# One bias product instead of sixteen, window attention scored one unit ahead, and a second early weight tile lowered after the norm

## The chip, the cores and the metric

The kernel is written in Bass for one core of a Trainium2 chip. It is one launch, and the metric is its device time in microseconds (us). The kernel before takes 3031.45 us, the median of three runs from 3026.38 to 3034.74. Five engines work beside one another and meet at semaphores: PE multiplies matrices, DVE and ACT do elementwise work, reductions and functions, POOL and SP here mostly issue DMAs.

## The reference, cut to what matters

The program computes two transformer blocks one after the other on 256 tokens of 1024 features. The first (`first_block`) has two layers, each a token mixer of three attention branches and a gated feed-forward with a convolution. The second has a gated delta-rule mixer, a SwiGLU feed-forward, a sliding-window attention with sinks and a bias by relative distance, and a mixture of eight experts with two chosen per token. The change touches the window attention and the two places where one stage hands over to the next.

```python
def swa_sink_attention(x, w_in, b_in, sinks, rel_bias, w_out):   # 16 query heads of 64, 2 key heads
    proj = x @ w_in + b_in
    ...
    s = jnp.einsum('bnqkgd,bnskd->bnkgqs', q, kb).astype(jnp.float32) * (SWA_HEAD_DIM ** -0.5)
    dist = qi + SWA_BLOCK - kj
    bias = rel_bias[t5_bucket(jnp.maximum(dist, 0))]             # rel_bias: 32 buckets x 16 heads
    band_ok = (dist >= 0) & (dist < SWA_WINDOW)                  # window of 128
    s = jnp.where(mask, s + bias, -jnp.inf)
    p = jax.nn.softmax(jnp.concatenate([s, sink], axis=-1), axis=-1)[..., :-1]
    o = jnp.einsum('bnkgqs,bnskd->bnqkgd', p, vb).reshape(bsz, t, SWA_QDIM)
    return o @ w_out
# between stages: x = layernorm(ALPHA * x + y); h = x * (1 + sc) + sh; next product h @ w
```

## The kernel before, in words

**Weights.** Every large product is made in three passes, so that it keeps fp32 accuracy on a faster format. A weight tile of 128x2048 comes from memory into one of four slots of `W` (SP issues the load), ACT copies it to a rounded "high" part (`raise_weight`, L1535), DVE subtracts to get the "low" part (`lower_weight`, L1953, two halves of 128x1024 per tile), and PE runs high x high, high x low, low x high (`product`, L805 to L807). PE hands the slot back when the tile is used. All engines run through the list of tiles in one order written by hand: `high(n)` and `low(n)` say where in ACT's and DVE's program the next n tiles are taken. At the end of a layer the first two tiles of the next stage are raised and lowered ahead of time, into free places of `arena` (`high_next`, `low_next(part, 2)`); the next stage's own list on DVE then starts behind these two.

**Handing over.** After the last product of a feed-forward (`down`, four results of 128x512), DVE adds each to x (`residual`), takes statistics, normalises (`norm`), PE transposes x in sixteen 128x128 pieces, and DVE and ACT scale and split the transposed x (`shifted` and `high_shifted`, two groups of four pieces, q = 0 and 1). Behind that DVE scales x itself (`scale_x`, four operations), and goes on to the next weight tiles. `shifted` takes a function that it calls after each group.

**The bias rows.** The bias of a head depends on the distance alone, so one row of 384 numbers per head describes it. In the middle stage, between the `up` and `down` products of the SwiGLU, PE multiplies for each of the 16 heads a 32x128 matrix, in which the head's 32 bucket values are repeated over 128 columns (`relspread`, made by DVE), with a 32x384 one-hot table. This gives the row 128 times. DVE adds the mask row to each (`add_row`, sixteen times, into `relw`). POOL writes the result, 16 heads x 128 partitions x 384 numbers, to `spread` in memory (L779), waits, and reads it back with a pitch of 383 per partition (L782), so that partition p gets the row shifted by p. The result is `wbias`; DVE waits for it (`bias_in`) before the window attention.

**The window attention.** There are 16 units: eight pairs of heads x two token blocks. The block t = 0 has 128 keys, the block t = 1 has 256. PE's program is, per unit u, the two score products of unit u (L980), the transposes of the probabilities of unit u-1 (L999), and the products with the values of unit u-2 (L1012). DVE's is: scale and bias the two score matrices of u (L2235), take the row maxima (L2241), take the maximum with the sinks, negate, subtract from the sinks (L2244, L2246, L2248), wait for ACT's exponentials of the same unit (L1596), add the sink's term and invert (L2997, L2999), and scale the result of unit u-2 (`w_out`, L2987). ACT's is: the exponential of the sinks (L1593), the two exponentials of unit u with their row sums, and the copy of the transposed probabilities of u-1 (L1520). `scores` and the small per-unit tiles have two buffers.

Banks of PSUM are given out in the order in which PE's program asks for them, eight in rotation; `JOBS` holds how many each stage uses.

## Time and profile before

| | |
|---|---|
| Time, median of three runs | 3031.45 us |
| The profiled execution | 3030.37 us, its span 3028.6 us |
| PE busy | 2732.2 us (90%) |
| DVE busy | 2177.5 us (72%) |
| ACT busy | 1508.3 us (50%) |
| Chain that ended last | PE 43%, DVE 21%, weight loads of PE 17%, issue 8%, ACT 7%, DMA 3% |
| Sixteen bias products | from 1729.14, 18.12 us |
| Window attention | from 1858.92 to 1929.49, 70.57 us |
| Residual after `down`, stage before layer 1 | starts at 691.37 |
| The same before the middle stage | starts at 1316.06 |

Times are counted from the start of the span. A matmul of PE is recorded with the weights and data that it reads; in full fp32 one product is recorded as two matmuls, so the sixteen bias products are 32. A busy PE is not a PE at its peak; the column PEclk gives the clock that the chip granted it, 1.00 for 2.4 GHz and 0.50 for 1.2 GHz. "[1.50 <-DVE small L2999]" behind a row means that the engine had been idle for 1.50 us until the DVE instruction of that line was done.

### The profile page before, as it was taken

To read this page: it belongs to the slowest core of one execution; us is meant where nothing else is said; L and a number is where in the kernel's file an instruction comes from. 1 tells how busy PE (TensorE), PEld (TensorE's weight loads), DVE (VectorE), ACT (ScalarE), POOL (GpSimd) and SP (SyncE) were. 2 spreads that over 40 slices of the span, in tenths; PEclk is the share of its full clock that TensorE was granted. 3 is DMA by queue.
4 is the path that set the end of the run, shared out by engine and by line. 5 is a ranking of instruction groups with operands and counts; after the bars stand their busy time and mean duration, and the time that the engine had idled before them with its cause. 6 is when DMAs were issued, how large, how long until landed. Compare 5 with 4: busy or idle time off the path is not lost.

```text
span 3028.6 us, 38615 instructions
## 1 busy us (share of the span) xinstructions
PE 2732.2 (90%) x14170; PEld 2319.9 (77%) x14170; DVE 2177.5 (72%) x2757; ACT 1508.3 (50%) x1773; POOL 24.4 (1%) x46
## 2 busy tenths in 40 slices
PE   8988798898887889987989997779999999999997
PEld 8777678886766679877889975668888888888886
DVE  1766577778756677665676646578889898898987
ACT  1333434533334345435333334447777777777774
POOL 0000000000000000000000000000000000000000
PEclk7989899999989999987999997679999999999999
DMA  6743345576633355442114462249889998898985
GB/s 248 271 165 135 119 156 205 205 262 244 228 129 125 114 192 204 166 148 85 56 56 164 167 234 86 98 180 367 338 339 362 343 368 337 336 363 342 370 336 222
DMA packets 104714, 671.13 MB, mean 222 GB/s; under 512 B 11984, under 2 KB 12240, under 8 KB 27136
## 3 DMA queue, kind: packets, MB, share of 16 engines
q1 hardware_dynamic: 97584, 622.08, 55.5%
q0 software_dynamic: 6992, 47.19, 4.2%
q8 instruction: 89, 1.46, 0.2%
q14 instruction: 49, 0.40, 0.0%
HBM read 665.03 MB, written 4.19 MB: 221 GB/s over the span
## 4 chain that ended last, share of the span: by engine, by line
PE 43%; DVE 21%; PEld 17%; issue 8%; ACT 7%; DMA 3%; PEldq 0%; DVEq 0%; ACTq 0%; SPq 0%
PE bank L805 12%; PE bank L806 11%; PE bank L807 11%; DVE W_low L1953 7%; PEld bank L807 5%; PEld bank L805 5%; PEld bank L806 5%; ACT W_high L1535 3%; PE bank L1189 3%; PE bank L939 2%; DMA W<-in_w_expert 2%; PE bank L862 1%; DVE work L2020 1%; PEld bank L1419 1%; DVE scores L2235 1%
## 5 line engine op out<-in xcount | busy, mean ns | idle before, releaser
L1953 DVE TENSOR_TENSOR W_low<-W,W_high 128x1024 fp32r<-128x1024 f32 x426 | 496.7, 1207 | 350.7 <-ACT W_high L1535 347.4
L1535 ACT ACTIVATE W_high<-W 128x1024 fp32r<-128x1024 f32 x426 | 421.8, 1039 | 479.4 <-PE bank L807 240.7
L806 PE MATMUL bank<-W_low,arena_parts 128*128 128x512 f32 x1288 | 506.5, 393 | 0.0
L805 PE MATMUL bank<-W_high,arena_parts 128*128 128x512 f32 x968 | 388.3, 401 | 10.1 <-DVE W_low L1953 5.8
L807 PE MATMUL bank<-W_high,arena_parts 128*128 128x512 f32 x968 | 381.9, 395 | 0.0
L807 PE MATMUL bank<-hT_high,W_low 128*128 128x256 f32 x1184 | 340.6, 288 | 0.0
L805 PE MATMUL bank<-hT_high,W_high 128*128 128x256 f32 x1072 | 312.4, 291 | 16.7 <-DVE W_low L1953 8.6
L805 PE MATMUL bank<-W_high,hT_high 128*128 128x512 f32 (+3 forms) x680 | 280.6, 413 | 35.6 <-DVE W_low L1953 12.1
L806 PE MATMUL bank<-hT_low,W_high 128*128 128x256 f32 x1072 | 307.5, 287 | 0.0
L806 PE MATMUL bank<-W_low,hT_high 128*128 128x512 f32 (+4 forms) x720 | 286.1, 397 | 0.0
L806 PEld LDWEIGHTS bank<-W_low,arena_parts 128*128 128x128 f32 x1288 | 244.4, 190 | 49.2
L805 PE MATMUL bank<-arena_parts 128*128 128x512 f32 x672 | 272.6, 406 | 1.9 <-DVE arena_parts L3110 1.9
L807 PE MATMUL bank<-W_high,hT_low 128*128 128x512 f32 (+3 forms) x680 | 270.1, 397 | 0.0
L807 PE MATMUL bank<-arena_parts 128*128 128x512 f32 x672 | 263.7, 392 | 0.0
L807 PEld LDWEIGHTS bank<-hT_high,W_low 128*128 128x128 f32 x1184 | 232.9, 197 | 0.0
L805 PEld LDWEIGHTS bank<-hT_high,W_high 128*128 128x128 f32 x1072 | 209.5, 195 | 23.5 <-DVE W_low L1953 13.5
L806 PE MATMUL bank<-arena_parts 128*128 128x512 f32 x576 | 225.5, 391 | 0.0
L805 PEld LDWEIGHTS bank<-W_high,arena_parts 128*128 128x128 f32 x968 | 184.4, 191 | 53.0 <-DVE W_low L1953 8.8
L1582 ACT ACTIVATE arena_parts<-W 128x2048 fp32r<-128x2048 f32 x96 | 184.3, 1920 | 76.5 <-DMA W<-in_w_expert 59.7
L1987 DVE TENSOR_TENSOR W_low<-W,arena_parts 128x2048 fp32r<-128x2048 f32 x96 | 218.0, 2285 | 2.8 <-ACT arena_parts L1582 2.8
L807 PEld LDWEIGHTS bank<-W_high,arena_parts 128*128 128x128 f32 x968 | 183.8, 190 | 40.1
L806 PEld LDWEIGHTS bank<-hT_low,W_high 128*128 128x128 f32 x1072 | 209.9, 196 | 0.1
(375 smaller groups left out, 4724.7 us busy)
## 6 DMA issues: line engine op xcount, KB each, us to landing
W<-in_w_expert SPq DMA_DIRECT2D x192, 1024.0 KB, 4.8
W<-in_w_layer SPq DMA_DIRECT2D x170, 1024.0 KB, 4.9
arena<-in_w_expert SPq DMA_DIRECT2D x144, 1024.0 KB, 4.8
W<-in_w_middle SPq DMA_DIRECT2D x58, 1024.0 KB, 4.8
arena<-in_w_layer POOLq DMA_DIRECT2D x40, 1024.0 KB, 6.1
R<-in_rows_layer SPq DMA_DIRECT2D x70, 256.0 KB, 5.8
R<-in_rows_middle SPq DMA_DIRECT2D x18, 256.0 KB, 5.5
spread<-arena POOLq DMA_DIRECT2D x1, 3072.0 KB, 13.7
```

Source lines behind the costliest of these rows:

```text
L805: mm(bank, lhs[0], rhs[0], start=start, stop=False)
L806: mm(bank, lhs[0], rhs[1], start=False, stop=False)
L807: return mm(bank, lhs[1], rhs[0], start=False, stop=stop)
L862: last = turn_over(bank[:, i * P:(i + 1) * P], src[:, t, f:f + P], ident)
L939: last = mm(bank[:, n:n + 1], part[:, a_:a_ + P], csil[:, f:f + 1], start=k == 0, stop=k == 3)
L1189: last = mm(bank[:, i * P:(i + 1) * P], lhs(i), rhs(i), start=True, stop=True)
L1419: last = turn_over(bank[:, i * P:(i + 1) * P], hid_tok[:, c % 2, i * P:(i + 1) * P], ident)
L1535: do(high_slot(at, w)[:, cols], raw(at, w)[:, cols], ACT.Copy).then_inc(main_highs.filled[main_highs.slot(at, w)], 1)
L1582: do(expert_high(j), expert_raw(j), ACT.Copy).then_inc(stream.raised, 1)
L1953: tt(lows(at, w)[:, cols], raw(at, w)[:, cols], high_slot(at, w)[:, cols].bitcast(F32), ALU.subtract).then_inc(*low_ready.event(at))
L1987: tt(expert_low(j), expert_raw(j), expert_high(j).bitcast(F32), ALU.subtract).then_inc(stream.lowered, 1)
L2020: i = stt(acc, part, csil[:, f:f + 1], acc, ALU.mult, ALU.add)
```

## The change

**Bias rows.** PE makes one product for all heads: the 32x16 table of bucket values as it came from memory against the one-hot table, 16x384. DVE adds the mask row once, on 16 partitions. The repetition over 128 partitions moves into the DMA that writes `spread`, whose source is now a broadcast of 16 partitions. `relspread` and its copy are gone.

**Window attention.** PE makes the scores of unit u+1 before it transposes the probabilities of u-1, DVE masks unit u+1 before it waits for the exponentials of unit u. Scores and the small tiles get three buffers of their own (`wscores`, `wmax`, `wsum`, `wsink`). DVE takes the maxima negated and takes the minimum with negated sinks, which were made once, so one of the three small operations is gone; ACT no longer waits between its three exponentials.

**Second early tile.** `low_next` lowers one tile ahead of time and no longer two. The second is lowered by `shifted` behind its second group (`low(q)` with q = 1), for layer 1 and for the middle stage. ACT still raises both early.

```diff
@@ the bias rows: POOL, PE, DVE
-            pool.dma_start(spread.rearrange("h p m -> p h m"), relw).then_inc(bias_out, 16)
+            pool.dma_start(spread, relrow[0:WQ_HEADS, :].unsqueeze(1).to_broadcast([WQ_HEADS, P, 384])
+                           ).then_inc(bias_out, 16)
...
-            for h_ in range(WQ_HEADS):
-                pe.wait_ge(*psum.vacant(at, ("rel", h_)))
-                bank = banks[psum.slot(at, ("rel", h_))]
-                mm(bank[:, 0:384], relspread[0:BUCKETS, h_, :], R[0:BUCKETS, hot, 0:384],
-                   start=True, stop=True).then_inc(*psum.fills(at, ("rel", h_)))
+            bank = banks[psum.slot(at, ("rel", 0))]
+            mm(bank[0:WQ_HEADS, 0:384], R[0:BUCKETS, relb, 0:WQ_HEADS], R[0:BUCKETS, hot, 0:384],
+               start=True, stop=True).then_inc(*psum.fills(at, ("rel", 0)))
...
-            for h_ in range(WQ_HEADS):
-                add_row(("rel", h_), r, relw[:, h_, :], width=384)
+            tt(relrow[0:WQ_HEADS, :], bank[0:WQ_HEADS, 0:384], r[0:WQ_HEADS, 0:384], ALU.add
+               ).then_inc(*psum.frees(v.at, ("rel", 0)))
@@ the window attention: PE
+            window_scores(0)
+            for u in range(16):
+                if u < 15:
+                    window_scores(u + 1)
+                if u:
+                    window_T(u - 1)
+                if u > 1:
+                    window_out(u - 2)
@@ ACT
+            def window_exps(u):
+                act.wait_ge(*masked.nth(a.at, u + 1))
+                K, b = (u % NT + 1) * P, u % 3
+                do(wsink[:, b, :], wsink[:, b, :], ACT.Exp)
+                for m in range(2):
+                    i = do(wscores[:, b, m, 0:K], wscores[:, b, m, 0:K], ACT.Exp,
+                           bias=wmax[:, b, m:m + 1], accum_out=wsum[:, b, m:m + 1])
+                i.then_inc(*exped.event(a.at))
@@ DVE
+            def window_mask(u):
+                hp, t = divmod(u, NT)
+                K, b = (t + 1) * P, u % 3
+                for m in range(2):
+                    job = ("Ws", hp, t, m)
+                    dve.wait_ge(*psum.full(v.at, job))
+                    bank = banks[psum.slot(v.at, job)]
+                    stt(wscores[:, b, m, 0:K], bank[:, 0:K], WD ** -0.5, wbias[:, 2 * hp + m, 2 * P - K:2 * P],
+                        ALU.mult, ALU.add).then_inc(*psum.frees(v.at, job))
...
+                V.reduce_max(wmax[:, b, :], wscores[:, b, :, 0:K], axis=AX, negate=True).then_inc(dve_done, 1)
+                tt(wmax[:, b, :], wmax[:, b, :], negative[:, 2 * hp:2 * hp + 2], ALU.min).then_inc(dve_done, 1)
+                tt(wsink[:, b, :], wmax[:, b, :], sinks[:, 2 * hp:2 * hp + 2], ALU.add).then_inc(*masked.event(v.at))
...
+            window_mask(0)
             for u in range(16):
-                mask("W", hp, t, u, 2, WD ** -0.5, lambda m, K: wbias[:, 2 * hp + m, 2 * P - K:2 * P])
+                if u < 15:
+                    window_mask(u + 1)
                 dve.wait_ge(*exped.nth(v.at, u + 1))
@@ the second early tile: DVE, end of layers 0 and 1, start of layer 1 and of the middle stage
-                low_next(LAYERS[l + 1] if l + 1 < DEPTH else "middle", 2)
+                low_next(LAYERS[l + 1] if l + 1 < DEPTH else "middle", 1)
...
-                    shifted("hT", modc[:, 80:88], modc[:, 88:96])
+                    shifted("hT", modc[:, 80:88], modc[:, 88:96], lambda q: low(q))
...
-            shifted("gxT", modc[:, 48:56], modc[:, 56:64])
+            shifted("gxT", modc[:, 48:56], modc[:, 56:64], lambda q: low(q))
```

DVE at the end of the middle stage's `up`, before; `arena<-bank,R` is the addition of the mask row, `W_low` a half of a weight tile lowered, `x<-x,bank` the residual after `down`:

```order
L2184 TENSOR_TENSOR acted<-acted,bank 128x256
L2186 CAST arena_parts<-acted 128x256
L2188 TENSOR_TENSOR arena_parts<-acted,arena_parts 128x256
L1943 TENSOR_TENSOR arena<-bank,R 128x384 x16
L1953 TENSOR_TENSOR W_low<-W,W_high 128x1024 x18
L1953 TENSOR_TENSOR W_low<-W,h_parts 128x1024 x2
```

The same of the changed kernel (its line numbers are its own):

```order
L2198 TENSOR_TENSOR acted<-acted,bank 128x256
L2200 CAST arena_parts<-acted 128x256
L2202 TENSOR_TENSOR arena_parts<-acted,arena_parts 128x256
L2947 TENSOR_TENSOR arena<-bank,R 16x384
L1967 TENSOR_TENSOR W_low<-W,W_high 128x1024 x18
L1967 TENSOR_TENSOR W_low<-W,h_parts 128x1024 x2
```

Sixteen additions on 128 partitions have become one on 16; the lowered tiles behind it stay.

PE in the window attention, before, two units from the third on; L980 are scores, L999 transposes, L1012 products with the values:

```order
L980 MATMUL bank<-arena 128x256 x2
L999 MATMUL bank<-consts,scores 128x128 x2
L1012 MATMUL bank<-arena,probsT 128x64 x4
L980 MATMUL bank<-arena 128x128 x2
L999 MATMUL bank<-consts,scores 128x128 x4
L1012 MATMUL bank<-arena,probsT 128x64 x2
```

The same of the changed kernel, with scores now at L981, transposes at L1000, products with the values at L1013:

```order
L981 MATMUL bank<-arena 128x128 x2
L1000 MATMUL bank<-consts,arena 128x128 x2
L1013 MATMUL bank<-arena,probsT 128x64 x4
L981 MATMUL bank<-arena 128x256 x2
L1000 MATMUL bank<-consts,arena 128x128 x4
L1013 MATMUL bank<-arena,probsT 128x64 x2
```

Before, the scores of a block with 256 keys stand ahead of the transposes of the unit just before it; now the scores of the block after that one (128 keys) stand there, one unit further ahead. The transposes read `wscores` in the arena.

DVE at the start of layer 1, before; `hT` and `hT_low` are the scaled and split transposes, `x<-x,R` is `scale_x`:

```order
L1973 TENSOR_SCALAR hT<-bank,modc 128x128 x4
L1980 TENSOR_TENSOR hT_low<-hT,hT_high 128x4x128 x2
L2146 TENSOR_TENSOR x<-x,R 128x2x512
L2148 TENSOR_TENSOR x<-x,R 128x2x512
L2146 TENSOR_TENSOR x<-x,R 128x2x512
L2148 TENSOR_TENSOR x<-x,R 128x2x512
L1953 TENSOR_TENSOR W_low<-W,W_high 128x1024 x2
```

The same of the changed kernel:

```order
L1987 TENSOR_SCALAR hT<-bank,modc 128x128 x4
L1994 TENSOR_TENSOR hT_low<-hT,hT_high 128x4x128 x2
L1967 TENSOR_TENSOR W_low<-W,arena_parts 128x1024 x2
L2160 TENSOR_TENSOR x<-x,R 128x2x512
L2162 TENSOR_TENSOR x<-x,R 128x2x512
L2160 TENSOR_TENSOR x<-x,R 128x2x512
L2162 TENSOR_TENSOR x<-x,R 128x2x512
L1967 TENSOR_TENSOR W_low<-W,W_high 128x1024 x2
```

The two halves of the second early tile (`W_low<-W,arena_parts`) now stand between the last split and `scale_x`; ahead of the residual they are gone. The middle stage has the same move.

## Rows read from the trace of the kernel before

**Rows 1.** The page, busy time of the engines.
```profile
PE 2732.2 (90%) x14170; PEld 2319.9 (77%) x14170; DVE 2177.5 (72%) x2757; ACT 1508.3 (50%) x1773; POOL 24.4 (1%) x46
```

**Rows 2.** Timeline of all engines around the bias products.
```profile
1729.14 18.12 PE L1338 MATMUL bank<-R,h 32*128 32x384 f32 x32 [0.30 <-PE bank L807]
1730.26 2.36 DVE L1953 TENSOR_TENSOR W_low<-W,W_high 128x1024 fp32r<-128x1024 f32 x2 [2.29 <-ACT W_high L1535]
...
1733.78 5.29 DVE L1943 TENSOR_TENSOR arena<-bank,R 128x384 f32<-128x384 f32 x9
...
1747.19 0.80 PE L805 MATMUL bank<-W_high,arena_parts 128*128 128x512 f32 x1
...
1752.43 0.39 PE L805 MATMUL bank<-W_high,arena_parts 128*128 128x512 f32 x1
1752.66 0.39 PE L806 MATMUL bank<-W_low,arena_parts 128*128 128x512 f32 x1
```

**Rows 3.** Busy time by stretch: stretch, length, busy PE, PEld, DVE, ACT, POOL, clock, DMA.
```profile
1733.00:1737.00 4.00, 4.00 (x8) 2.15 (x7) 3.76 (x8) 0.00 (x0) 0.00 (x0) 0.50 0.03 12
1747.00:1752.00 5.00, 5.00 (x12) 3.81 (x12) 0.56 (x1) 0.00 (x0) 1.18 (x1) 0.50 0.38 140
```

**Rows 4.** The tile `spread`: POOL's issue of the write, and both DMAs.
```profile
L779 POOL DMA_DIRECT2D spread<-arena x1: 1181/1181/1181, 1748.3 to 1748.3; - x1
...
DMA to landing us min/median/max: 12.2/13.0/13.7
```

**Rows 5.** Timeline of all engines, window attention: its start, two units, its end.
```profile
1858.92 0.93 PE L980 MATMUL bank<-arena 64*128 64x128 f32 x8 [0.88 <-ACTq L1523]
...
1870.73 0.69 PE L999 MATMUL bank<-consts,scores 128*128 128x128 f32 x2 [0.43 <-DVE small L2999]
...
1871.04 0.88 DVE L2235 SCALAR_TENSOR_TENSOR scores<-bank,arena 128x256 f32<-128x256 f32 x2
...
1874.84 0.16 DVE L2997 TENSOR_TENSOR small<-small 128x2 f32<-128x2 f32 x1 [1.61 <-ACT scores L1596]
...
1875.56 0.62 DVE L2235 SCALAR_TENSOR_TENSOR scores<-bank,arena 128x128 f32<-128x128 f32 x2
...
1877.06 0.16 DVE L2248 TENSOR_TENSOR small<-R,small 128x2 f32<-128x2 f32 x1
...
1929.49 3.68 PE L862 MATMUL bank<-consts,arena 128*128 128x128 f32 x16 [0.60 <-DVEq L3006]
```

**Rows 6.** Busy time by stretch, as rows 3: four units of the window attention.
```profile
1870.70:1887.30 16.60, 12.08 (x52) 9.58 (x52) 9.51 (x36) 7.14 (x25) 0.00 (x0) 0.50 0.00 0
```

**Rows 7.** Timeline of DVE, end of layer 0 and start of layer 1.
```profile
684.88 2.36 DVE L1953 TENSOR_TENSOR W_low<-W,arena_parts 128x1024 fp32r<-128x1024 f32 x2 [0.82 <-ACT arena_parts L1535]
689.09 2.36 DVE L1953 TENSOR_TENSOR W_low<-W,arena_parts 128x1024 fp32r<-128x1024 f32 x2 [1.85 <-ACT arena_parts L1535]
691.37 0.68 DVE L2164 TENSOR_TENSOR work<-bank,arena 128x512 f32<-128x512 f32 x1
...
710.04 1.22 DVE L2146 TENSOR_TENSOR x<-x,R 128x1024 f32<-128x1024 f32 x1
...
715.07 2.36 DVE L1953 TENSOR_TENSOR W_low<-W,W_high 128x1024 fp32r<-128x1024 f32 x2
```

**Rows 8.** Timeline of PE, the same place.
```profile
691.99 0.39 PE L807 MATMUL bank<-W_high,arena_parts 128*128 128x512 f32 x1
701.49 3.40 PE L862 MATMUL bank<-consts,x 128*128 128x128 f32 x16 [9.11 <-DVE x L2130]
706.39 0.47 PE L805 MATMUL bank<-arena_parts,hT_high 128*128 128x512 f32 x1 [1.50 <-DVE hT_low L1980]
...
717.54 0.40 PE L805 MATMUL bank<-W_high,hT_high 128*128 128x512 f32 x1
```

**Rows 9.** Timeline of DVE, end of layer 1 and start of the middle stage.
```profile
1313.78 2.36 DVE L1953 TENSOR_TENSOR W_low<-W,arena_parts 128x1024 fp32r<-128x1024 f32 x2 [2.17 <-ACT arena_parts L1535]
```

**Rows 10.** Timeline of PE, the same place.
```profile
1320.14 0.39 PE L807 MATMUL bank<-W_high,arena_parts 128*128 128x512 f32 x1
```

More of the change, by code:

```diff
@@ L129 @@
 ARENA = 22544
-JOBS = {'start': 0, 'layer0': 200, 'layer1': 192, 'middle': 281, 'expert': 37, 'last': 35, 'over': 37, 'end': 0}
+JOBS = {'start': 0, 'layer0': 200, 'layer1': 192, 'middle': 266, 'expert': 37, 'last': 35, 'over': 37, 'end': 0}
 GIVEN = {
@@ L2259, in _ @@
                 state["std"] = 0
-                state["group"], state["split"] = 0, iter(SPLIT[LAYERS[l]][2 if l else 0:])
+                state["group"], state["split"] = 0, iter(SPLIT[LAYERS[l]][1 if l else 0:])
                 if not l:
@@ L2655, in _ @@
             v.enter("middle")
-            state["std"], state["group"], state["split"] = 0, 0, iter(SPLIT["middle"][2:])
-            shifted("gxT", modc[:, 48:56], modc[:, 56:64])
+            state["std"], state["group"], state["split"] = 0, 0, iter(SPLIT["middle"][1:])
+            shifted("gxT", modc[:, 48:56], modc[:, 56:64], lambda q: low(q))
             for n in range(2):
```

81 lines of the change are left out of this document (34 added, 47 removed).

## Prediction, made before the changed kernel ran

> **What bounds the kernel now.** I read the page first, to see which engine is full. PE is busy for 90% of the span, DVE for 72%, ACT for 50% [rows 1]. This says that a saving counts where PE itself loses work, or where PE waits. It does not say which: the shares are means over many stages. So I went to the three places that the diff touches and read each from the timeline, asking what PE does there and what ends its waits.
>
> At the bias products PE doesn't wait, it works: 32 recorded matmuls take 18.12 us, from 1729.14, and the next product (`down`) starts at 1747.19 [rows 2]. During them the granted clock is 0.50, with PE busy for all of the stretch; it is still 0.50 while `down` begins [rows 3]. DVE's sixteen additions run beside them [rows 2]. So PE is the bound of this stretch and the products are a pure addition to the time.
>
> In the window attention PE is busy 12.08 us in 16.60 us for four units, DVE 9.51, ACT 7.14 [rows 6]. No engine is full: the unit goes round a ring. DVE masks unit u, waits 1.61 us for ACT's exponentials of that same unit, inverts, and only then does PE transpose [rows 5]. The period is 16.60 / 4 = 4.15 us per unit, and it is a latency. The clock is 0.50 here too.
>
> At the two handovers PE waits for DVE. Before layer 1 it is idle 9.11 us until the normalised x is there [rows 8]. DVE reaches the residual at 691.37 only after lowering two early tiles, and it had stood 1.85 us idle for ACT ahead of the second [rows 7]. Before the middle stage the second tile also has DVE idle first, for 2.17 us [rows 9].
>
> **The bias rows.** Removed on PE are 15 of 16 products, 30 of 32 recorded matmuls. The two that stay cost 2 x 18.12 / 32 = 1.1 us, so `down` can start at 1729.14 + 1.1 = 1730.3 instead of 1747.19: 16.9 us. It needs its first tile lowered, and DVE is then already at the next one, done at 1730.26 + 2.36 = 1732.6 [rows 2]; PE asks for that tile after 24 matmuls of 0.23 us (the distance of the last two rows of rows 2), at 1735.8. Further on the loads, ACT and DVE are paced by the slots that PE hands back, as before. Second, `down` began on the slow clock: its first 12 matmuls took 1752.43 - 1747.19 = 5.24 us, against 12 x 0.23 = 2.76 at the full clock, 2.5 us more. The product ahead, `up`, ran up to 1729, so with two sparse matmuls between I expect the clock to stay. Sum 16.9 + 2.5 = **19.4 us**; it is 16.9 if the clock falls all the same, and at most 20.6 if the two matmuls vanish.
>
> DVE loses fifteen additions, hidden behind PE today and worth nothing on their own; that the sixteenth works on 16 partitions is worth nothing either. The copy into `relspread` is hidden in the same way. The bucket row is released later than before, but its successor in that slot is a row for the norm after `down`.
>
> What the change adds is in the DMA. The write of `spread` now reads 16 partitions 128 times over; no row of the trace shows such a source. It can be issued at about 1733.78 + 0.6 = 1734.4 and its reader is DVE at the start of the window attention, at 1858.92 - 19.4 = 1839.5 in the new time [rows 2, 5]. So 105 us cover it and the reading back, which take 13.7 and at least 12.2 us now [rows 4]. POOL has nothing queued behind these two. Bounds: no quicker than nothing, which gives nothing since it is hidden, and free up to 105 - 13.7 = 91 us for the write, nearly seven times today's. I take zero. It shares the DMA engines with the weights of `down`, and did so before.
>
> The Trainium skill ("SBUF — State Buffer", section on the DMA port swizzle) speaks against this edit: partitions 0 to 15 reach only four of sixteen ports, measured there at 104 GB/s. The write moves 3.1 MB, so an estimate from that page is 30 us. With it the sum stays the same, since the cover is larger; no run here shows it yet.
>
> **The window attention.** Work per engine and unit in the new order, from the same rows. DVE's mask for 256 keys goes from 1871.04 to 1874.84 - 1.61 = 1873.23, 2.19 us; for 128 keys from 1875.56 to 1877.06 + 0.16 = 1877.22, 1.66 us [rows 5]. One of three small operations goes, at 0.2 us each, which leaves 1.99 and 1.46. Sum, reciprocal and `w_out` together take 1875.56 - 1874.84 = 0.72 us. The mean is (1.99 + 1.46) / 2 + 0.72 = 2.45 us a unit. ACT has 7.14 / 4 = 1.8, PE 12.08 / 4 = 3.02 [rows 6]. The ring is open: while ACT does unit u, DVE masks u+1, and PE has the scores of u+1 behind it. With a unit of distance more, the probabilities of u are ready some 3.5 to 4 us after its scores, and PE comes to transpose it two turns, 6 us, later. So the longest engine sets the pace: PE, 3.02 us.
>
> The start: the first mask can begin about 0.6 us after the start, masks 0 and 1 end at 4.1, unit 0 is inverted at 4.5, mask 2 ends at 6.0, unit 1 is ready for its transposes at 6.4. From there PE has work without a gap. Of its 16 x 3.02 = 48.3 us it has then done the scores of four units and one transpose, and the last product stands behind a wait; together about 6.5. That leaves 41.8, to 48.2. The last copy of probabilities, the last products, and `w_out` follow with about 3.3 us, as they do today. The total is 51.5 us instead of 1929.49 - 1858.92 = 70.57 [rows 5]: **19.1 us**. Bounds: zero, if every unit still closes its ring, and 24.5, if PE were not the longest: then DVE sets 2.45 us for 14 units, and 6.4 + 34.3 + 4.4 for the end gives about 45 to 46. I take 19.1 because the PE row is the one measured in this very loop, at the clock that it had there.
>
> About this clock the skill ("TensorE: Matmul & The Clock Gate", Part 1) says that throttling is the resting state and sustained activity of PE lifts it. That would give the attention the full clock once its gaps close, and the result of 24.5. The trace doesn't follow the plain form of it: in rows 3 PE is busy 4.00 of 4.00 us at 0.50. I keep it as a rival.
>
> **The second early tile.** Before layer 1, DVE is free at 684.88 + 2.36 = 687.2 and can start the residual 4.1 us earlier than 691.37. The four results of `down` are there when asked for: PE ends at 692.4 [rows 8] and finishes one every 12 x 0.23 = 2.76 us, so 684.1, 686.9, 689.6, 692.4; DVE takes about 2.2 us each and comes to the last at 694. The normalised x comes 4.1 us earlier, and the idle 1.85 us is gone. The 2.36 us of lowering now stand behind the last split, ahead of `scale_x` and whatever is queued there. PE needs the second tile's first half after 24 matmuls from 706.39 - 4.1, at 707.8; DVE has it at 710.04 - 4.1 + 1.2 = 707.1. That holds by 0.7 us. The next tile comes later relative to PE: it starts at 715.07 - 4.1 + 2.36 = 713.3, its first half is there at 714.5, and PE wants it at 717.54 - 4.1 = 713.4 [rows 7, 8]. PE waits 1.1 us. The gain is 4.1 - 1.1 = **3.0 us**. If DVE bounds what follows it is only the idle time, 1.85; if the wait is recovered, 4.1.
>
> Before the middle stage the first early tile is tiny, and DVE is free at 1313.78 - 2.17 = 1311.6. The last result of `down` comes at 1320.5 [rows 10], so there DVE starts the fourth residual instead of at 1316.06 + 3 x 2.2 + 0.3 = 1322.9. That is **2.4 us**. The lowering behind the split then eats what DVE has won, and `scale_x` ends when it does now; PE starts with a narrow product that uses the other tile. I take all of it, with zero as the lower end, if a step of DVE behind `scale_x` is what the stage waits for.
>
> **Sum.** 19.4 + 19.1 + 3.0 + 2.4 = 43.9 us. All of it lies ahead of the experts, whose loads SP issues only after the attention's result is split, so nothing behind can give it back or absorb it: the later part moves as a whole. 3030.37 - 43.9 = 2986.5 for the profiled execution, which lay 1.1 us under the median of the runs: 2987.5. I say **2987 us**.
>
> **The rivals.**
> 1. The clock rises in the attention (the rule above). For it: PE will have no gaps there, and its products use all 128 rows more often than the bias products did. Against: rows 3. It gives 24.5 instead of 19.1, so 2982.
> 2. The attention's period stays well above PE's work, say 3.6 us, since one of PE's in-order waits still falls on a late engine. For it: DVE's 2.45 leaves out most semaphore time. Against: 0.6 us of room per unit. 14 x 0.6 = 8 us less: 2995.
> 3. The handovers give nothing: DVE or row loads bound both starts. For it: layer 1 goes straight on at DVE at 715.07 without a pause [rows 7]. 5.4 us less: 2993.
> 4. Slower than before: the write from sixteen partitions chokes the DMA engines while `down` needs its weights. `down` uses a tile every 24 x 0.23 = 5.5 us over eleven tiles. If the write took eight times its 13.7 us, 110 us, and halved the rate of the weight loads throughout, each tile would come 5 us late, 55 us in all: 2987 + 55 = 3042. It turns the sign once the write costs `down` over 44 us. For it: the source has an eighth of the partitions. Against: the write before shared the engines with the same loads and PE ran on, and only a source slower than anything in the trace reaches this.
>
> **How the numbers follow.** Forecast 0.53, rival 1 0.2, rival 2 0.12, rival 3 0.1, rival 4 0.03, something else 0.02. The forecast and rivals 1 to 3 lie between 2982 and 2995; with the bounds of the terms (16.9 for the bias, 4.1 at layer 1) and the 4 us by which runs of this kernel differ from their median, the range is 2976 to 3001. A change within 0.3%, 9 us, is what I count as none; it takes the loss of four fifths of the sum, 0.02. Slower has rival 4 and a little for the unknown, 0.03. Faster 0.95.
>
> **What would show it.** One L1338 group of two matmuls, `down` starting within 2 us behind it at clock 1.00; PE's transposes in the attention with idle times near zero and a period near 3.0, or 2.5 with the clock at 1.00; the attention 51 to 52 us long; the residual before layer 1 starting 4 us earlier relative to the end of `down`, then about 1 us of PE waiting for `W_low` at the third tile; the write of `spread` landing long before DVE asks. The prediction is wrong if the attention keeps DVE idle for ACT, if `down` shows gaps on weight loads, or if a stretch behind the attention grows.

## The result, and the profile after

The changed kernel takes 2992.8 us (median of 4 runs, 2990.95 to 3003.66), the kernel before beside it 3029.4 us (median of 4, 3026.38 to 3034.74). The ratio is 0.988, its 95% interval 0.987 to 0.990: 1.2% faster. The forecast was 2987 us in a range of 2976 to 3001. The profiled execution took 2991.22 us (span 2989.4) against 3030.37 (span 3028.6): 39.2 us less, where the sum of the terms said 43.9.

Since both executions are timelines of the same work, the difference can be split at points that both have. Such a point is a product that starts a stage.

| stretch, and the points it runs between | before, us | after, us | difference | forecast |
|---|---|---|---|---|
| start to the first product of layer 1 | 706.39 | 701.22 | -5.2 | |
| layer 1, to the late wait inside its `down` | 603.86 | 605.07 | +1.2 | |
| (these two together) | | | -4.0 | -3.0 |
| handover to the middle, from there to its first product | 24.61 | 22.10 | -2.5 | -2.4 |
| middle, up to the bias products | 394.28 | 393.15 | -1.1 | 0 |
| bias products, `down`, projections, up to attention | 129.78 | 116.49 | **-13.3** | **-19.4** |
| window attention | 70.57 | 50.19 | -20.4 | -19.1 |
| attention's output to the first expert product | 74.20 | 74.11 | -0.1 | 0 |
| experts and end | 1024.9 | 1027.1 | +2.2 | 0 |

Of the first row 0.5 us was there before anything in the program differed. Three terms are as forecast within some 1.3 us. One is short by 6.1 us, and 2.2 us come back at the end. The 1.1 us of the middle stage were in no term.

The page, busy time of the engines, as [rows 1]:

```profile
PE 2714.3 (91%) x14140; PEld 2309.3 (77%) x14140; DVE 2162.2 (72%) x2726; ACT 1504.7 (50%) x1773; POOL 24.2 (1%) x46
```

PE has lost 30 matmuls and 18 us of work; the other 21 us are idle time. Now the bias rows, timeline of all engines, the place of [rows 2] (start, length, engine and line, then the operation; in brackets the idle time ahead and what ended it):

```profile
1721.54 0.80 PE L1338 MATMUL bank<-R 32*16 32x384 f32 x2 [0.30 <-PE bank L808]
1722.27 0.50 PE L806 MATMUL bank<-W_high,arena_parts 128*128 128x512 f32 x1
...
1726.17 0.55 DVE L2947 TENSOR_TENSOR arena<-bank,R 16x384 f32<-16x384 f32 x1
1727.07 1.05 POOL L779 DMA_DIRECT2D spread<-arena  x1 [542.60 <-DVEq L2950]
...
1744.85 0.50 PE L806 MATMUL bank<-W_high,arena_parts 128*128 128x512 f32 x1 [0.51 <-DVE W_low L1967]
...
1754.31 0.50 PE L806 MATMUL bank<-W_high,arena_parts 128*128 128x512 f32 x1 [3.71 <-DVE W_low L1967]
...
1755.40 0.63 PE L807 MATMUL bank<-W_low,arena_parts 128*128 128x512 f32 x1
1755.83 0.63 PE L808 MATMUL bank<-W_high,arena_parts 128*128 128x512 f32 x1
```

Two matmuls stand where 32 stood, and `down` starts 0.73 us behind the first of them, on the full clock. So far this is the forecast. But inside `down` PE now waits 0.51 and 3.71 us for a lowered weight tile; there was no such wait at these places before. Behind the second wait the products are 0.43 us apart instead of 0.23. Busy time by stretch (stretch, length, busy PE, PEld, DVE, ACT, POOL, then the granted clock, DMA busy share, GB/s), as [rows 3]:

```profile
1722.40:1732.00 9.60, 9.60 (x43) 7.91 (x44) 6.32 (x8) 3.39 (x5) 1.05 (x1) 1.00 0.60 143
1742.00:1752.00 10.00, 8.09 (x35) 6.04 (x33) 2.36 (x2) 2.07 (x3) 0.00 (x0) 1.00 1.01 245
1752.00:1762.00 10.00, 7.69 (x27) 6.08 (x28) 4.25 (x4) 3.95 (x4) 0.00 (x0) 0.83 0.99 256
```

What DVE waited for is ACT, and what ACT waited for stands in the waits of 1722 to 1792 (engine, tile and line, what it waited for, us in total, times, longest):

```profile
DVE W_low L1967 <- ACT W_high L1543: 35.8, 10, 7.1
POOL arena L783 <- DMA spread<-arena: 35.0, 1, 35.0
ACT W_high L1543 <- DMA W<-in_w_middle: 22.3, 4, 7.5
```

ACT waited 22.3 us for weight loads. In the view of before that starts with its `down` (1747 to 1812), ACT's waits were 27.4 us for PE and none for a load. The DMAs between 1727 and 1763 show the reason (packets of each queue, MB, share of the 16 DMA engines; issues with KB and median us to landing):

```profile
q0 software_dynamic: 704, 3.15, 63.4%
q1 hardware_dynamic: 642, 4.74, 31.2%
...
W<-in_w_middle SPq DMA_DIRECT2D x6, 1024.0 KB, 17.0
spread<-arena POOLq DMA_DIRECT2D x1, 3072.0 KB, 35.8
```

and of before, 1748.3 to 1762, the write of the same 3 MB:

```profile
q0 software_dynamic: 704, 3.15, 67.7%
q1 hardware_dynamic: 133, 1.02, 19.9%
...
spread<-arena POOLq DMA_DIRECT2D x1, 3072.0 KB, 13.7
```

The write takes 35.8 us instead of 13.7 [rows 4]. Its packets held the engines for 0.634 x 36 x 16 = 365 engine-microseconds, against 0.677 x 13.7 x 16 = 148 before, for the same bytes. The loads' own packets did not get dearer: 0.312 x 36 x 16 / 4.74 = 38 engine-microseconds per MB, against 0.199 x 13.7 x 16 / 1.02 = 43 before. So the write is not only late itself: while it runs, a weight load lands in 17.0 us, and the loads get 4.74 MB / 36 us = 132 GB/s where `down` uses one tile of 1.05 MB in some 5.44 us, 193 GB/s.

Window attention, timeline of PE, one pair of units:

```profile
1852.40 0.69 PE L1000 MATMUL bank<-consts,arena 128*128 128x128 f32 x2
1852.88 1.80 PE L1013 MATMUL bank<-arena,probsT 128*128 128x64 f32 x8
1854.61 1.23 PE L981 MATMUL bank<-arena 64*128 64x256 f32 x4
1855.77 1.11 PE L1000 MATMUL bank<-consts,arena 128*128 128x128 f32 x4
1856.67 0.95 PE L1013 MATMUL bank<-arena,probsT 128*128 128x64 f32 x4
1857.56 0.80 PE L981 MATMUL bank<-arena 64*128 64x128 f32 x4
1858.29 0.69 PE L1000 MATMUL bank<-consts,arena 128*128 128x128 f32 x2
```

and busy time by stretch, 16.6 us of it, as [rows 6]:

```profile
1852.40:1869.00 16.60, 16.60 (x76) 13.61 (x74) 11.20 (x44) 8.49 (x35) 0.00 (x0) 0.50 0.00 1
```

No transpose here carries a wait, where the one of [rows 5] waited 0.43 us for DVE; in the whole stage those of two units wait, of sixteen before. A pair takes 1858.29 - 1852.40 = 5.89 us instead of 8.30; PE is busy all of it, at clock 0.50. At the two handovers PE's rows, as [rows 8, 10], are:

```profile
696.52 3.48 PE L863 MATMUL bank<-consts,x 128*128 128x128 f32 x16 [4.65 <-DVE x L2144]
701.22 0.47 PE L806 MATMUL bank<-arena_parts,hT_high 128*128 128x512 f32 x1 [1.23 <-DVE hT_low L1994]
...
713.45 0.50 PE L806 MATMUL bank<-W_high,hT_high 128*128 128x512 f32 x1 [0.94 <-DVE W_low L1967]
...
728.30 0.79 PE L806 MATMUL bank<-W_high,hT_high 128*128 128x512 f32 x1 [2.28 <-DVE W_low L1967]
...
1319.96 2.22 PE L863 MATMUL bank<-consts,x 128*128 128x128 f32 x16 [3.39 <-DVE x L2144]
```

PE's wait ahead of the transposes is 4.65 us where it was 9.11, and 3.39 where it was 5.66. The second time the sixteen transposes take 2.22 us instead of 3.38 (timeline of PE, before):

```profile
1326.18 3.38 PE L862 MATMUL bank<-consts,x 128*128 128x128 f32 x16 [5.66 <-DVE x L2130]
```

The clock had not fallen here; it had in one other kernel behind the same wait of 3.39 us (the product made 16 times, below), where they took 3.59 us.

### The profile page after: what moved, and what is told of

Same layout as the page of the kernel before. It is cut to its first block, busy times and chain, and to the rows that moved or that the text cites. A ratio compares the mean times of both kernels' runs of the same rounds, so it can differ in the third digit from the quotient of the medians.

```text
span 2989.4 us, 38477 instructions
## 1 busy us (share of the span) xinstructions
PE 2714.3 (91%) x14140; PEld 2309.3 (77%) x14140; DVE 2162.2 (72%) x2726; ACT 1504.7 (50%) x1773; POOL 24.2 (1%) x46
## 4 chain that ended last, share of the span: by engine, by line
PE 44%; DVE 20%; PEld 16%; issue 8%; ACT 7%; DMA 3%; PEldq 0%; DVEq 0%; ACTq 0%; SPq 0%
PE bank L806 12%; PE bank L807 11%; PE bank L808 11%; DVE W_low L1967 7%; PEld bank L808 5%; PEld bank L806 5%; PEld bank L807 5%; ACT W_high L1543 3%; PE bank L1190 3%; PE bank L940 2%; DMA W<-in_w_expert 1%; PE bank L863 1%; DVE work L2034 1%; PEld bank L1427 1%; PE bank L1013 1%
## 5 line engine op out<-in xcount | busy, mean ns | idle before, releaser
L806 PE MATMUL bank<-W_high,hT_high 128*128 128x512 f32 (+3 forms) x680 | 282.7, 416 | 36.8 <-DVE W_low L1967 14.8
L806 PEld LDWEIGHTS bank<-W_high,arena_parts 128*128 128x128 f32 x968 | 183.9, 190 | 57.8 <-DVE W_low L1967 13.9
L806 PEld LDWEIGHTS bank<-hT_high,W_high 128*128 128x128 f32 x1072 | 209.0, 195 | 23.6 <-DVE W_low L1967 13.9
## 6 DMA issues: line engine op xcount, KB each, us to landing
spread<-arena POOLq DMA_DIRECT2D x1, 3072.0 KB, 35.8
```

What stands on the lines that cost most here:

```text
L806: mm(bank, lhs[0], rhs[0], start=start, stop=False)
```

## The experiments

Theory 1: the write from 16 partitions holds the DMA engines 2.5 times as long, and the weight loads under it come too late for `down`. The rival: what made the write harmless before was a pause, 18 us in which PE used up no weights and the loads ran ahead. Each kernel was run beside the kernel before, on the same chip; the ratio is to that. Since executions of one kernel differ by some microseconds long before the places in question, two times are read from the traces too: the stretch from the bias product to attention (129.78 us before), and attention itself (70.57 us). All are in this table; "write" is the time from the issue of the write to its landing (13.7 us before).

| kernel | median, us | ratio (95% interval) | write, us | waits of PE in `down`, us | stretch, us | attention, us |
|---|---|---|---|---|---|---|
| bias edit alone | 3024.0 | 0.997 (0.996 to 0.998) | 36.6 | 0.47, 5.72 | 119.56 | 70.6 |
| attention edit alone | 3015.4 | 0.995 (0.993 to 0.996) | 13.5 | none | 129.8 | 50.2 |
| early tile edit alone | 3026.8 | 0.999 (0.998 to 1.000) | 13.6 | none | 129.8 | 70.6 |
| changed, 128 source partitions | 2990.0 | 0.986 (0.984 to 0.988) | 18.7 | none | 109.90 | 50.2 |
| changed, 16 copies | 2988.3 | 0.985 (0.983 to 0.987) | 5.5 | none | 109.83 | 50.2 |
| changed, write later | 2997.4 | 0.988 (0.986 to 0.990) | 34.5 | none (9.05 behind it) | 117.19 | 50.2 |
| changed, product 16 times | 3021.3 | 0.997 (0.995 to 0.998) | 35.8 | 7.80 | 139.43 | 50.2 |
| changed, attention in the old order | 3007.6 | 0.992 (0.991 to 0.994) | 36.0 | 2.36, 1.35, 1.36 | 117.48 | 60.6 |
| changed, longer chain | 2997.3 | 0.989 (0.987 to 0.991) | 36.7 | 3.85, 1.52 | 117.63 | 51.5 |
| changed, no early tile | 2995.8 | 0.988 (0.986 to 0.990) | 36.6 | 0.18, 4.28 | 116.35 | 50.2 |
| changed, once more | 2995.0 | 0.987 (0.985 to 0.989) | 35.8 | 0.95, 3.28 | 116.63 | 50.2 |
| changed, both mends | 2988.6 | 0.985 (0.983 to 0.987) | 3.7 | none | 109.91 | 50.2 |

(The waits of 1.05 and 0.17 us at the end of `down`, which all kernels have, are left out.)

### The three edits, each alone

Each is the kernel before with only those lines of the diff that belong to one edit.

> The kernel before with the bias edit alone: one product, one add, and the write of the score rows to DRAM from 16 partitions. Theory 1 (the write starves the weight loads of the middle down): the write lasts 30 to 40 us where it lasted 13.7, weight loads that overlap it land in about 17 us, PE stands idle some 4 us for a lowered weight tile inside down and its clock falls, so that of the 19.4 us forecast for this term some 13 are left: 3016 us against 3029.4 before. Rival 1 (the term is as forecast, and the missing microseconds of the whole change lie elsewhere, or come only with the early start that the other edits give): 3010 us, no gap in down. Rival 2 (the 16-partition write is so slow that it costs more than the products gave): 3030 us or more.

> The kernel before with the window attention alone changed (a unit ahead, three score buffers, the shorter chain for the sink). Theory 1: PE becomes the bound at about 2.95 us a unit instead of 4.4, attention lasts 50 us instead of 70.6, and the kernel takes 3009 us. Rival (the attention's gain is in part the gift of another edit, the clock or the DMA state at its start): 3015 us or more, with a longer stage than the 50.2 us in the changed kernel.

> The kernel before with only the second early weight tile moved behind the norm, at both handovers. Theory 1: 3.5 us at layer 1 and 2.5 to 3.6 us at the middle, 3023 us in all. Rival (the lowering that is moved comes back as waits of PE in the stage behind, nothing is left): 3029 us.

The bias edit alone gained 129.78 - 119.56 = 10.2 us in its stretch, a little over half of its term, with PE waiting inside `down` (timeline of PE):

```profile
1754.49 0.50 PE L804 MATMUL bank<-W_high,arena_parts 128*128 128x512 f32 x1 [0.47 <-DVE W_low L1951]
...
1765.99 0.80 PE L804 MATMUL bank<-W_high,arena_parts 128*128 128x512 f32 x1 [5.72 <-DVE W_low L1951]
```

So the loss belongs to this edit and needs no help from the earlier start that the others give; the first rival falls. By its median it came out at 3024, 8.5 us below its neighbours, and not at the 3016 expected: the expectation took 6 us for the loss, which is 9.2 in the stretch here, and knew nothing of the 2.3 us that come back at the end (below). The attention edit alone made the same 50.2 us and a ratio that fits, and the early tile 22.11 us for the handover to the middle, as in the changed kernel, and 5.7 us by the medians (an interval of 0.05 to 0.24%). There is no sign that the three need each other. Their gains by the medians, 8.5, 17.1 and 5.7 us, add up to 31.3, against the 36.6 us of all three (both times from the kernel before beside each). Of the difference 3.1 us are the bias edit's stretch (10.2 alone, 13.3 with the others), and 2.2 are the end, which the first two each pay in full.

### 128 source partitions

```diff
-            pool.dma_start(spread, relrow[0:WQ_HEADS, :].unsqueeze(1).to_broadcast([WQ_HEADS, P, 384])
+            pool.dma_start(spread.rearrange("h (r j) m -> (h r) j m", r=8),
+                           relrow.unsqueeze(1).to_broadcast([P, P // 8, 384]))
-            mm(bank[0:WQ_HEADS, 0:384], R[0:BUCKETS, relb, 0:WQ_HEADS], R[0:BUCKETS, hot, 0:384],
+            mm(bank[:, 0:384], R[0:BUCKETS, relb, 0:P], R[0:BUCKETS, hot, 0:384],
-    relb[:BUCKETS, :WQ_HEADS] = i["rel_bias_2"]
+    relb[:BUCKETS, :P] = np.repeat(i["rel_bias_2"], 8, axis=1)
```

> The changed kernel with the 16 columns of the bias table laid out eight times each, so that the one product gives 128 partitions (row of a head on eight of them) and the write to DRAM reads from 128 partitions, sixteen copies each: the same 3 MB to the same place. Theory 1 (few source partitions make the write slow, and the slow write starves the weight loads): the write lands in 14 to 18 us again, the two gaps of PE in down (0.51 and 3.71 us) go, about 6 us are saved: 2986.5 us. Rival (it is the missing pause: before, the weight loads had 18 us of idle PE to run ahead in; any 3 MB write right behind up starves them): the write takes 20 us or more beside the loads, PE still waits 3 to 5 us in down: 2990 to 2993 us.

The same bytes now land in 18.7 us, with no pause ahead of them. DMAs from 1729.7 to 1748.7:

```profile
q0 software_dynamic: 704, 3.15, 46.2%
q1 hardware_dynamic: 442, 3.23, 41.9%
...
W<-in_w_middle SPq DMA_DIRECT2D x4, 1024.0 KB, 8.2
spread<-arena POOLq DMA_DIRECT2D x1, 3072.0 KB, 18.7
```

The write costs 0.462 x 19.0 x 16 = 140 engine-microseconds, as before the change (148), and the loads get 3.23 MB / 19.0 us = 170 GB/s. PE does not wait in `down`, and the stretch is 109.90 us: 19.9 less than before the change, where the forecast said 19.4. The whole loss of the term is back. This is what theory 1 gives and the rival doesn't, which had 3 to 5 us of waiting in `down`. Nor does the order in memory decide: each partition writes its 16 copies next to one another here and wrote its 16 rows 196 KB apart before, and both are quick. The median alone, 2990.0 us, would not have decided: theory 1 said 2986.5, the rival 2990 to 2993.

### The product sixteen times: the pause put back

```diff
+            for _ in range(16):
+                last = mm(bank[0:WQ_HEADS, 0:384], R[0:BUCKETS, relb, 0:WQ_HEADS], R[0:BUCKETS, hot, 0:384],
+                          start=True, stop=True)
```

> The changed kernel with the one product of the bias rows made sixteen times over into the same bank, so that PE is again busy some 15 to 18 us before down while no weights are used up, and the write still goes from 16 partitions. Theory 1 (the narrow source alone makes the write slow): it lands in about 30 to 36 us again, not 14, and since it lasts longer than the loaded tiles, PE still waits in down, 1 to 6 us. Rival (the pause is what made the write of the kernel before harmless and short): the write lands in 14 to 20 us and down has no gap. Time 3008 to 3013 us by theory 1, 3004 to 3008 by the rival.

The other corner of the square: the pause (18.12 us of products, as before) with the narrow source. The write lands in 35.8 us, and PE waits longer than ever (timeline of PE):

```profile
1771.10 0.80 PE L806 MATMUL bank<-W_high,arena_parts 128*128 128x512 f32 x1 [7.80 <-DVE W_low L1969]
```

The pause doesn't shorten the write and doesn't save `down`. Nor is it a matter of when the write begins: POOL issues it 1.1 us behind the start of `down`, as before the change, and 4.8 us behind it in the changed kernel. With the loads run ahead, the trace also has 16 us in which the write moves nearly alone (DMAs from 1743 to 1759):

```profile
q0 software_dynamic: 351, 1.62, 95.9%
...
q1 hardware_dynamic: 1, 0.01, 0.1%
```

That is 1.62 MB / 16 us = 101 GB/s with the engines counted busy for 96%: the write is slow by itself, not by the loads beside it. And they are late by it: the load that SP issued at 1747.01 moved next to nothing before 1758. The stretch is 139.43 us, 9.7 more than before the change with the same products on PE. That is the price of the narrow source by itself. The time was missed: 3021 by the median, though the profiled execution took 3014.9 and the runs lie between 3015 and 3027, for theory 1's 3008 to 3013; so was the wait, 7.80 us for 1 to 6.

### Sixteen copies instead of 128

```diff
+            pool.dma_start(spread[:, 0:16, :], relrow[0:WQ_HEADS, :].unsqueeze(1).to_broadcast([WQ_HEADS, 16, 384])
+            for r in range(8):
+                shifted = bass.AP(spread.tensor, P - 1 - r, [[376, 16], [P * 384, WQ_HEADS], [1, S]])
+                pool.dma_start(wbias[r::8], shifted).then_inc(bias_in, 16)
```

> The changed kernel with sixteen copies of each score row in DRAM instead of 128: the write is 0.4 MB from the same 16 partitions, and the read is made in eight parts, each of 16 partitions eight apart, 2 MB in all as before. Theory 1 (bytes through few partitions are what is slow, 35.8 us for 3 MB): the write lands in 5 to 7 us, the weight loads land within 10 us, no gap of PE in down, 2986 us, as with 128 source partitions. Rival (the number of transfers beside the loads matters, and eight reads are no better): the reads take over 25 us or PE waits in down, 2990 us or more.

Another way to the same end: the source stays narrow, an eighth of the bytes is written. It lands in 5.5 us, the eight reads behind it (last issue 1742.1) in 12.8 us by the median and 24.2 at most. The reads are close to the rival's 25 us, and the weight loads between 1730 and 1770 took 11.2 us by the median, not under 10, but no wait came of it in `down`: a stretch of 109.83 us, 2988.3 us against the 2986 of the expectation. So bytes times slowness is what counts, not the narrow source as such.

### The write later

`bias_made` is signalled eight lowered tiles further on in `down` (whole tiles, not the half tiles that the expectation names): the write is issued 46 us behind the start of `down` instead of 4.8.

> The changed kernel with the write of the score rows released eight lowered half tiles into the middle down, some 40 us later, where fewer weight loads are left. Theory 1 (the slow write starves whatever loads lie under it): down has no gap in its first 40 us, but the write, 25 to 36 us from about 1765, now lies under the loads of the query weights; what it costs there is 0 to 4 us, and the read ends some 20 us before attention: 2987 to 2992 us. Rival (the loss of down comes from something else at its start, such as the missing pause): the two gaps of 0.5 and 3.7 us stay where they are, 2993 us.

The two waits in `down` are gone, which rules out anything else at its start, but the write costs as much at the new place (timeline of PE, then waits of 1785 to 1810):

```profile
1802.92 0.77 PE L806 MATMUL bank<-h_parts,hT_high 128*128 128x512 f32 x1 [9.05 <-DVE hT_low L1994]
```

```profile
DVE hT_low L1994 <- ACT hT_high L1570: 8.2, 2, 7.5
ACT W_high L1543 <- DMA W<-in_w_middle: 7.0, 1, 7.0
```

The starved load stood ahead of the activations in ACT's order: ACT waited 7.0 us for a tile, and the raising of the activations, for which PE waited, was queued behind that. The mechanism was right, its size was not: 7 to 8 us against the 0 to 4 expected, and 2997 us.

### Attention in the old order, and with the longer chain

The first takes the unit ahead out of PE's and DVE's loops and keeps three buffers, the shorter chain and the exponential of the sink without its wait. The second keeps the order and puts the fifth operation (a negation) back on DVE.

> The changed kernel with the order of the kernel before in window attention (scores of a unit are not made a unit ahead) but with three score buffers and the shorter chain of four operations for the sink. Theory 1 (the round trip PE to DVE to ACT to DVE to PE bounds a unit, and only the order takes it off the path): a pair of units takes about 8.1 us where it took 8.30, attention lasts 67 to 69 us, 3010 us in all. Rival (the buffers and the shorter chain give much of it): 60 us or less, 3003 us.

> The changed kernel with the longer chain of the kernel before for the sink (maximum, maximum with the sink, negate, add) put back, five operations a unit on DVE's way to the exponentials, while scores stay a unit ahead. Without the order but with the short chain a pair of units took 7.08 us. Theory 1 (a unit ahead, PE alone bounds the pair, 5.89 us, and DVE has about half a microsecond a unit to spare): the longer chain is hidden, attention stays at 50.2 us, the kernel within 1 us of the changed one (ratio 0.988). Rival (the short chain is needed to stay within PE's time): the pair takes over 6.1 us, attention over 52 us.

Timeline of PE in the old order, the transposes that begin two pairs, and busy time by stretch with the longer chain, two pairs:

```profile
1870.57 1.12 PE L1000 MATMUL bank<-consts,arena 128*128 128x128 f32 x4 [0.89 <-DVE small L3015]
...
1877.64 1.12 PE L1000 MATMUL bank<-consts,arena 128*128 128x128 f32 x4 [0.89 <-DVE small L3015]
```

```profile
1852.20:1864.20 12.00, 11.91 (x54) 9.57 (x52) 8.77 (x36) 6.04 (x24) 0.00 (x0) 0.50 0.00 0
```

My theory for the first was wrong and the rival nearly right: a pair takes 1877.64 - 1870.57 = 7.07 us (8.1 expected), attention 60.6. Half of the 20.4 us comes without the order, 0.6 us a unit. The operations taken out of the ring explain part of that: one of DVE's, at 0.16 us, and ACT's exponential of the sink, 0.20 us, on whose end the others had waited; the rest was not told apart. The order gives the other 10.4 us. In the new order the fifth operation costs 1.3 us in all, between no cost (theory 1) and the rival's 2: 0.4 us pass ahead of the first transposes, and PE's gaps are then 0.1 us in 12.

### No early tile

Both early tiles are lowered inside the shifted norm, one behind each half.

> The changed kernel with the first early weight tile too moved from ahead of the residual to behind the first half of the shifted norm at both handovers, so that DVE lowers nothing between the last weight tile of down and the residual. Theory 1 (DVE is the chain at the handover until the norm is done, and PE needs the first lowered tile with its first product): the transposes start 2.35 us earlier, but the lowering of 2.35 us now stands between the two halves of the shifted norm, on the way to the same first product; nothing at layer 1, 0 to 1 us lost at the middle: ratio 0.988 to 0.989. Rival (the first product waits only for the first half, the gain of the second tile can be had again): 2 to 4 us faster, ratio 0.987.

The transposes start 3.39 us after the end of `down` instead of 4.65, and the first product of layer 1 then waits 3.17 us for its weight tile where it waited 1.23 for `hT_low`. From the last transposes of layer 0 (L971) to the first product of layer 1 it is 22.03 us, against 21.44 to 22.10 in the ten kernels with one early tile, and 26.11 before. At the middle it is 22.38 us against 22.10 to 22.27. Nothing is left to win, as theory 1 said.

### The changed kernel once more, and both mends together

Here the source has 128 partitions and each writes two copies of its row.

> The changed kernel itself once more, as the measure for the run beside it on the same chip. The scatter of the starve: the write lands in 34 to 37 us, PE waits 2 to 6 us in the middle down for lowered weight tiles, ratio 0.987 to 0.989. It would speak against the theory if down had no gap here with the write as slow as that.

> The changed kernel with both mends together: the product gives 128 partitions (eight for each head), each of them writes two copies of its row, sixteen for each head, 0.4 MB; the read is made in eight parts. Theory 1 (the starve is gone with either mend, and nothing is left to win from the other): as with either, product to attention 109.8 us, no gap in down, 4 to 7 us less than the changed kernel beside it, ratio 0.985 to 0.986. Rival (either mend left some of it): under 109 us for that stretch, and more than 8 us less than the changed kernel.

On one chip the changed kernel took 2995.0 and the mended one 2988.6 us, 6.4 us less; the interval of its ratio (0.983 to 0.987) still touches that of the changed kernel (0.985 to 0.989), so the number is carried by the trace: 109.91 us for the stretch against 116.63, and no wait in `down`. The two mends don't add up, since either takes all of the loss. The version with sixteen copies and the one with both are the fastest here, 1.5% below the kernel before.

## Why the prediction was right, and where it failed

**The verdict and the time.** Faster, and 2992.8 us inside the range, 5.8 us above the number. In the profiled executions the sum is 4.7 us too large: 6.1 by the bias rows and 2.2 by the end, and 3.6 us of small gains in the other rows of the table make up for a part. That these cancel is luck: none of them was in the forecast.

**The bias rows, 19.4 us, came out at 13.3.** The step that failed is "It shares the DMA engines with the weights of `down`, and did so before", with "I take zero". I had compared the write's landing with its reader, which is 105 us away, and found 91 us of cover. The cover was real: the write landed at 1763 and the read at 1778, 60 us ahead of attention. But the write's landing was the wrong end to look at. It has neighbours with far less cover, the weight loads, of which `down` wants one every 5.4 us, and it takes engine time from them, 365 engine-microseconds instead of 148. The forecast's rival 4 had this very mechanism, and I gave it 0.03 since I priced it only where it turns the sign. Below that point I had let it cost nothing; it cost 6. The words of the Trainium skill ("SBUF — State Buffer", section on the DMA port swizzle) were the better guide: few partitions reach few ports. Its figure of 104 GB/s gave an estimate of 30 us; 34.5 to 36.7 were measured in the eight kernels with this write, 101 GB/s where it moved nearly alone, and 18.7 us from 128 partitions under the same loads. What I did wrong was to apply the rule to the write alone. The other steps of the term held: the two matmuls cost 0.7 us for 1.1, and `down` began at clock 1.00 (its first 12 matmuls took 2.9 us for 5.2, so 2.4 us for 2.5). With a source of 128 partitions the term is 19.9.

Of the 6.6 us between the changed kernel's stretch and the 109.90 us, 6.4 lie between the bias product and the transposes behind `down`. Waits for the tiles are 0.51 + 3.71 = 4.2 of them. The clock, which fell some 1 us behind the second wait, took eight products at 0.43 instead of 0.23 us, 1.6. The rest, some 0.5 us, lies around the two waits, where the first product behind each takes 0.33 us instead of 0.23. Another 0.45 us is in the transposes, which took 3.34 us here and 2.23 with the wide source, behind the same wait of 2.67 us; that is not the write's doing as far as the runs show, since they took 2.22 us in the kernel without an early tile, which has the slow write too. The rest of the stretch is 0.2 us shorter in the changed kernel.

**The attention, 19.1 us, came out at 20.4.** The pace is PE's, as argued, 2.95 us a unit for the 3.02 of [rows 6]; the stage took 50.19 us for 51.5. Sixteen times the 0.07 us is 1.1 of the 1.3 us by which it is shorter. The clock did not rise: 0.50 with PE busy 16.60 of 16.60 us. In the bias products of before it even fell, from 1.00 to 0.50, with PE busy for all of the 18.05 us (busy time by stretch, before):

```profile
1729.14:1747.19 18.05, 18.05 (x33) 9.11 (x33) 11.77 (x20) 2.24 (x3) 0.00 (x0) 0.58 0.17 58
```

Rival 1 is false here, and of the rule of the Trainium skill ("TensorE: Matmul & The Clock Gate", Part 1), that sustained activity lifts the throttle, the trace shows that PE without a gap isn't enough in this stage. Rival 2 is false too. In explaining the period as one open ring I had the right end, but half of the gain needs no reordering, and my expectation before the run in the old order shows that I did not know it.

**The early tile.** At layer 1 the residual started at 686.40, right behind the one early tile, and the first product 4.65 us earlier for 4.1. The wait at the third tile was forecast at 1.1 us and is 0.94; a later one grew by the same again, from 1.18 to 2.28. The net gain is 3.5 us over the layer for the 3.0 forecast, though layer 1 alone differs between executions by more than that (602.1 to 608.4 us from its first product to the late wait in `down`, over the fourteen kernels, without order by edit). At the middle it is 2.5 us, for 2.4 (22.10 to 22.27 us in the ten kernels with one early tile, against 24.55 to 24.68 in three without it). Another 0.65 us up to 1390 is the clock: at 0.50 from the stage's first product in both kernels, it came back to 1.00 at 13.9 us behind that product instead of 14.8, and sooner once more around 1373 (1380 before), for 0.2 us. What sets that moment was not tested. Rival 3 is false.

**"Nothing behind can give it back"** was wrong by 2.2 us, and not in the experts. The distances between their steps are the same to 0.1 us. It is the last norm: DVE stands idle before its first statistics (timeline of DVE, before, then after):

```profile
3013.87 1.42 DVE L2108 BATCH_NORM_STATS2 small<-x 128x6 f32<-128x512 f32 x2 [1.88 <-issue]
```

```profile
2974.72 1.42 DVE L2122 BATCH_NORM_STATS2 small<-x 128x6 f32<-128x512 f32 x2 [4.19 <-issue]
```

It waited for nothing that the profile shows. The idle time is 1.88 us in the kernel before and with the early tile edit alone, and 4.08 to 4.38 us in the twelve others, all of which have another number of DVE instructions. The traces have one more thing that goes with it. In the twelve kernels an 8 KB packet of an instruction queue (q14) starts 1.8 to 2.0 us ahead of the first statistics, inside the idle time; in the two others no packet of that queue lies between 4.4 us ahead of them and 0.6 us behind. So DVE may have waited for instructions, fetched at another moment for where the code now lies; that is a guess, and no run tested it.

## What to carry to other kernels

A DMA off the critical path isn't free until its neighbours on the DMA engines have been counted: price it by the engine time it takes from the loads that run under it, at the partitions it reads from, and not by the time until its reader. When a product shrinks to few output partitions, look at what reads that tile next; repeating columns of the stationary operand up to 128 kept the product at 0.88 us for two matmuls instead of 0.80 and the DMA quick. And where a rival has the right mechanism but not the size to turn the sign, put its small version into the sum.

## What the runs showed of the hardware that I had not expected

- The same 3.15 MB to DRAM took 13.7 us from 128 partitions, 18.7 us from 128 under more load, and 34.5 to 36.7 us from 16, in the latter case whether loads ran beside it for nearly all of that time or for the second half alone (35.8 us each).
- While the slow write ran, the DMA engines counted as busy 0.95 to 1.01 and moved 220 GB/s; with the wide source they were busy 0.88 and moved 336. Nearly alone, the narrow write kept them busy for 0.96 of the time at 101 GB/s. A high busy share of DMA says that packets are held, not that bytes move.
- The clock: a wait of 3.71 us in `down` was followed, some 1 us later, by products at half speed (granted clock 0.83 over 10 us). A wait of 3.39 us ahead of the middle was followed by quick transposes in the changed kernel (2.22 us) and by slow ones in the kernel with the product made 16 times (3.59); one of 2.67 us behind `down` by slow ones in the changed kernel (3.34) and quick ones with 128 source partitions (2.23). So the length of the wait alone doesn't tell.
- PE busy without a gap doesn't keep the clock up either: it fell from 1.00 to 0.50 within the 18.05 us of the sixteen bias products, and in attention it stayed at 0.50 over 40 us (1848 to 1888) with PE busy for 39.0.
